# Gate products of the feed-forward by seven half-sized products instead of eight

## The chip, the cores and the metric

One core of a Trainium2 chip runs the whole program. The metric is device time in microseconds (us): the kernel before takes 1422.29 us, the median of 3 runs (1422.12 to 1422.38).

## The reference, cut to what matters

Two transformer-like blocks over 512 tokens of width 1024, in fp32. The change is in the last part of the second block, its gated feed-forward with 2816 hidden features:

```python
x = x + merged @ w_out[layer]
h = rmsnorm_2(x, norm_ffn[layer])
x = x + (jax.nn.silu(h @ w_ffn_gate[layer]) * (h @ w_ffn_up[layer])) @ w_ffn_down[layer]
```

Every large product must hold fp32 accuracy. `h @ w_ffn_gate` is 512 x 1024 times 1024 x 2816.

## The kernel before

**Products.** Everything is kept transposed: features on the 128 partitions, the 512 tokens in the free dimension, so a 1024-wide activation is 8 tiles of 128x512. Weights arrive in slabs of 1024 x 256 (8 inner tiles of 256 columns, 1 MB). A slab is split into two fp32r numbers: ScalarE writes the rounded high part (`split_hi`, L1146), VectorE the rest (`split_lo`, L1695); activations are split the same way. A product of two split numbers is three matmuls, high x high, high x low and low x high (`gemm`, L467). A slab gives two blocks of 128 outputs; a block is 8 inner tiles x 3 = 24 matmuls of 512 columns into one PSUM bank, and a slab is 48.

**Rings.** The raw slab, its high part and its low part each have 2 buffers. A slab is loaded when the low part of the slab two before is written, and split when TensorE has left the slab two before. SyncE issues all weight loads in program order.

**The end of `wout` (L2290 on VectorE, L1611 on ScalarE).** Four slabs, blocks k = 0 to 7. After each block VectorE adds it to the residual x (`add_to_x`, L2283), ScalarE multiplies x by the norm's gain and rounds it to `n_hi` (L1615) and squares x (L1603), VectorE writes the rest `n_lo` (L2288), GpSimd adds the squares (L2424). The root of their mean is needed only later, since the norm's factor is multiplied into the outputs (`RSTD`). TensorE starts the first feed-forward slab at once (`fup_part`, L1050): inner tiles 0 to 6 of both its blocks (42 matmuls), and only then tile 7 of both.

**The feed-forward.** Gate slab and up slab alternate (`fup0`, `fup1`, `fup2`: 4, 4 and 3 pairs), VectorE and ScalarE make silu(gate) x up of each and split it (L2316 to L2327), and after each chunk of 8 hidden tiles come the down slabs (`fdown0`, `fdown1`, each 4 slabs). The last 6 hidden tiles are `fdown2` and `fdown_end`; the last one's blocks are done by halves of 256 tokens (`end_block`, L1083).

**Order.** Each engine's program is written out by hand and an engine waits in order, on semaphores: what stands behind a waiting instruction waits as well.

Of the kernel before, what the change touches and what calls it, by code (L numbers as in the profile page):

```python
# [114 lines left out]
def build(nc, a, out):  # L115
# [79 lines left out]

    PH, s_at, b_at = {}, 0, 0
    for name, n, bps in [("in", 14, 2), ("pool_out", 2, 4), ("conv_out", 2, 4), ("wo", 4, 2)] + \
# [140 lines left out]
    def _(sp):
# [107 lines left out]
        run("fdown_end", w_d, k0=2 * KT, c0=3 * SLAB, kts=6)
# [9 lines left out]
    def _(pe):  # L456
# [587 lines left out]
        s0, _, b0, _ = PH["fup0"]  # L1044
        pe.wait_ge(S("lo_done"), s0 + 1)

        def fup_part(b, k):

            for n, (w, x) in enumerate(((hi_of, NHI), (hi_of, NLO), (lo_of, NHI))):
                mm = nc.tensor.matmul(G[(b0 + b) % 4][:], w(s0)[:, k, P * b:P * b + P], x[:, k, :],  # L1050
                                      start=k == 0 and n == 0, stop=k == KT - 1 and n == 2)
            return mm

        for b in range(2):
            pe.wait_ge(evac[(b0 + b) % 4], (b0 + b) // 4 + 1)
            for k in range(KT - 1):
                pe.wait_ge(S("ffn_in_lo"), k + 1)
                fup_part(b, k)
# [9 lines left out]
        gemm(s0 + 1, b0 + 3, range(KT), P, h(NHI), h(NLO))
        run("fup0", h(NHI), h(NLO), lo_slab=2, slabs=6)
        run("fup1", h(NHI), h(NLO))  # L1070
        run("fdown0", h(EHI[0]), h(ELO[0]), ready=h_ready(fbase))
        run("fup2", h(NHI), h(NLO))
        run("fdown1", h(EHI[1]), h(ELO[1]), ready=h_ready(fbase + KT))
        run("fdown2", h(EHI[0]), h(ELO[0]), kts=range(6), ready=h_ready(fbase + 2 * KT))

        def end_block(q):
# [1482 lines left out]
```

## Time and profile before

| what | value |
|---|---|
| median of 3 runs | 1422.29 us |
| the profiled execution's own time | 1422.33 us |
| its span in the trace | 1420.4 us |
| TensorE matmul busy | 1404.3 us, 99% of the span, 7223 matmuls |
| VectorE busy | 786.2 us, 55%, 1130 instructions |
| ScalarE busy | 538.5 us, 38%, 773 instructions |
| GpSimd busy | 167.1 us, 12% |
| TensorE clock granted, mean | 0.997 of full |

The times of instructions are from the start of the span. A matmul's listed duration (0.39 us for 512 columns) is longer than its pace, since one is under way while the next starts; the pace is the distance of two starts. On VectorE and ScalarE too an instruction may start some 0.08 us before the one ahead of it is listed as ended.

### The profile page before, as it was taken

Reading aid. Unit: us, or ns where it says so; the run is one execution under the profiler, and the core shown is the slowest. Engines: PE = TensorE matmul, PEld = TensorE weight load, DVE = VectorE, ACT = ScalarE, POOL = GpSimd, SP = SyncE. Lnnn points to the kernel's source line nnn. Section 1 sums busy time; section 2 is a strip of 40 time slices with the busy share of each in tenths; the row PEclk is TensorE's granted clock in tenths of the full one; section 3 lists DMA queues with packets and bytes.
Section 4 is the critical chain, followed back from the end, with each engine's and each line's share of the span. In section 5 each row is a group of like instructions: output and inputs, shape, how many; then the busy total and the mean of one; then the engine's idle time right before and its main releaser. Section 6 shows DMA issues by size and latency. Waiting matters only on the chain.

```text
span 1420.4 us, 17501 instructions
## 1 busy us (share of the span) xinstructions
PE 1404.3 (99%) x7223; PEld 1142.9 (80%) x7223; DVE 786.2 (55%) x1130; ACT 538.5 (38%) x773; POOL 167.1 (12%) x163
## 2 busy tenths in 40 slices
PE   7999999999999999999999999999999999999998
PEld 6888788988888888888888776668888888888887
DVE  6998674744234343378474666764545555435423
ACT  6232434643333132255453436662343223212214
POOL 1040013100000000120131711112210000000002
PEclk9999999999999999999999999999999999999999
DMA  6322224112322332323243212112322332332221
GB/s 200 116 89 90 89 89 148 61 60 89 119 89 90 101 103 92 96 90 97 89 90 119 73 60 60 30 31 76 103 90 89 108 100 90 97 111 89 90 89 60
DMA packets 136014, 129.67 MB, mean 91 GB/s; under 512 B 15776, under 2 KB 131424, under 8 KB 135904
## 3 DMA queue, kind: packets, MB, share of 16 engines
q1 hardware_dynamic: 134800, 124.90, 28.3%
q0 software_dynamic: 992, 3.47, 0.8%
q8 instruction: 57, 0.93, 0.3%
q10 hardware_dynamic: 144, 0.20, 0.0%
q14 instruction: 21, 0.17, 0.0%
HBM read 126.06 MB, written 2.10 MB: 90 GB/s over the span
## 4 chain that ended last, share of the span: by engine, by line
PE 95%; ACT 2%; DVE 1%; DMA 1%; issue 1%; SPq 0%; ACTq 0%
PE gemm L467 75%; PE gemm L586 3%; PE gemm L969 2%; PE misc L990 2%; PE misc L1009 1%; PE gemm L670 1%; PE gemm L617 1%; PE gemm L1050 1%; PE gemm L982 1%; PE misc L818 1%; DMA w_raw<-in_w_in 1%; PE misc L617 1%; PE gemm L495 1%; PE misc L982 1%; PE gemm L1083 1%
## 5 line engine op out<-in xcount | busy, mean ns | idle before, releaser
L1695 DVE TENSOR_TENSOR w_lo<-w_raw,w_hi 128x2048 fp32r<-128x2048 f32 (+1 forms) x108 | 245.8, 2276 | 174.6 <-ACT w_hi L1146 174.6
L467 PE MATMUL gemm<-h_hi,w_hi 128*128 128x512 f32 x828 | 324.8, 392 | 0.0
L467 PE MATMUL gemm<-h_hi,w_lo 128*128 128x512 f32 x828 | 322.3, 389 | 0.0
L467 PE MATMUL gemm<-h_lo,w_hi 128*128 128x512 f32 x828 | 322.3, 389 | 0.0
L1146 ACT ACTIVATE w_hi<-w_raw 128x2048 fp32r<-128x2048 f32 (+1 forms) x113 | 213.9, 1893 | 143.9 <-PE gemm L467 139.5
L467 PEld LDWEIGHTS gemm<-h_hi,w_hi 128*128 128x128 f32 x828 | 155.4, 188 | 35.2 <-issue 2.4
L467 PEld LDWEIGHTS gemm<-h_hi,w_lo 128*128 128x128 f32 x828 | 155.4, 188 | 32.6
L467 PEld LDWEIGHTS gemm<-h_lo,w_hi 128*128 128x128 f32 x828 | 155.5, 188 | 31.7 <-issue 0.2
L467 PE MATMUL gemm<-n_hi,w_hi 128*128 128x512 f32 x336 | 130.9, 390 | 0.0
L467 PE MATMUL gemm<-n_lo,w_hi 128*128 128x512 f32 x336 | 130.7, 389 | 0.0
L467 PE MATMUL gemm<-n_hi,w_lo 128*128 128x512 f32 x336 | 130.7, 389 | 0.0
L2424 POOL TENSOR_TENSOR sq_sum<-sq_sum,sq 128x512 f32<-128x512 f32 (+1 forms) x27 | 38.8, 1438 | 708.4 <-ACT sq L1603 365.3
L467 PE MATMUL gemm<-f_hi,w_hi 128*128 128x512 f32 x304 | 118.3, 389 | 0.0
L467 PE MATMUL gemm<-f_lo,w_hi 128*128 128x512 f32 x304 | 118.3, 389 | 0.0
L467 PE MATMUL gemm<-f_hi,w_lo 128*128 128x512 f32 x304 | 118.3, 389 | 0.0
L1785 DVE SCALAR_TENSOR_TENSOR conv_out<-v_padded,conv_cols,conv_out 128x512 f32<-128x512 f32 x120 | 89.8, 807 | 0.5
L467 PEld LDWEIGHTS gemm<-n_hi,w_hi 128*128 128x128 f32 x336 | 63.1, 188 | 13.3 <-issue 0.2
L467 PEld LDWEIGHTS gemm<-n_hi,w_lo 128*128 128x128 f32 x336 | 63.1, 188 | 13.1
L467 PEld LDWEIGHTS gemm<-n_lo,w_hi 128*128 128x128 f32 x336 | 63.1, 188 | 12.9
L467 PEld LDWEIGHTS gemm<-f_hi,w_lo 128*128 128x128 f32 x304 | 57.1, 188 | 11.9
L467 PEld LDWEIGHTS gemm<-f_hi,w_hi 128*128 128x128 f32 x304 | 57.1, 188 | 11.8
L467 PEld LDWEIGHTS gemm<-f_lo,w_hi 128*128 128x128 f32 x304 | 57.1, 188 | 11.8
(472 smaller groups left out, 1940.8 us busy)
## 6 DMA issues: line engine op xcount, KB each, us to landing
w_raw<-in_w_in SPq DMA_DIRECT2D x62, 512.0 KB, 4.6
w_raw<-in_w_down SPq DMA_DIRECT2D x32, 512.0 KB, 4.0
w_raw<-in_w_up SPq DMA_DIRECT2D x28, 512.0 KB, 4.3
w_raw<-in_w_ffn_gate SPq DMA_DIRECT2D x22, 512.0 KB, 4.5
w_raw<-in_w_ffn_up SPq DMA_DIRECT2D x22, 512.0 KB, 4.4
w_raw<-in_w_ffn_down SPq DMA_DIRECT2D x16, 512.0 KB, 4.2
w_raw<-in_w_o SPq DMA_DIRECT2D x8, 512.0 KB, 4.1
w_raw<-in_w_out SPq DMA_DIRECT2D x8, 512.0 KB, 4.1
```

The source lines that it names most:

```text
L467: mm = nc.tensor.matmul(bank[:], w(s)[:, kt, col0:col0 + P], x(n), start=first, stop=last)
L495: nc.tensor.matmul(G[(m + b) % 4][:], w(s)[:, k, P * b:P * b + P], HHI[:, k, :], start=k == 0 and w is hi_of, stop=False)
L586: mm = nc.tensor.matmul(G[m % 4][:], wide(w(s0 + j))[:, k, P * b:P * b + P], x[:, k, :], start=k == 0 and n == 0, stop=k == 3 and n == 2)
L617: mm = nc.tensor.matmul(bank[:, 0:HALF], w(s)[:, n // 3, P * (q % 2):P * (q % 2) + P], x[:, n // 3, SIDE[q // 2]], start=n == 0, stop=n == 23)
L670: nc.tensor.matmul(G[(m + b) % 4][:, SIDE[half]], w(s + b // 2)[:, k, P * (b % 2):P * (b % 2) + P], HHI[:, k, SIDE[half]], start=half == 0 ...
L969: mm = nc.tensor.matmul(G[bl % 2][:], w(s)[:, kt, P * (bl % 2):P * (bl % 2) + P], y[:, kt, :], start=x % 24 == 0, stop=x % 24 == 23)
L982: nc.tensor.matmul(banks[g][:, 0:w + P], QT[rows, q, w:w + P], KR[rows, i, 0:w + P], start=True, stop=True).then_inc(S("scores_full"), 1)
L990: mm = nc.tensor.transpose(bank[:, kb * P:(kb + 1) * P], PB[q % 2][:, g, kb * P:(kb + 1) * P], IDENT[:])
L1146: nc.scalar.activation(part(hi_of(s), s), part(raw_of(s), s), ACT.Copy).then_inc(S("hi_done"), SLABS_AT[s])
L1695: V.tensor_tensor(part(lo_of(s), s), part(raw_of(s), s), f(part(hi_of(s), s)), SUB).then_inc(S("lo_done"), SLABS_AT[s])
L1785: ins = V.scalar_tensor_tensor(y, x, w, y, MUL, ADD)
L2424: Q.tensor_tensor(SQA[:, cols], SQA[:, cols], SQ[j % 2][:, cols], ADD).then_inc(S("sq_added"), 1)
```

## The change

The 1024 x 256 gate slab is treated as a 2 x 2 matrix of halves: inner tiles even or odd, output columns 0 to 127 or 128 to 255. The activations are halved by the same inner tiles and by tokens 0 to 255 or 256 to 511. The four result quarters come from seven products in place of eight (Winograd's form): product p takes a half of the activations or a sum of such halves, and a half of the slab or a sum of such halves, 4 inner tiles x 3 = 12 matmuls of 256 columns each, 84 in all. The up and down slabs keep their products (48 matmuls of 512 columns to a slab).

Added around it:
- sums of the activations: 4 per pair of inner tiles (`input_sums`), once, in the `wout` loop. The activations now exist as 8 things to split (`ffn_in_hi`, `ffn_in_lo`), and ScalarE first writes x times gain in fp32 (`x_gained_pair`), then rounds it;
- sums of the weights: 4 operations per gate slab (`weight_sums`), three to `ffn_sums`, one in place in the raw slab, and the split of `ffn_sums` (1536 columns);
- sums of the products: ScalarE copies product 1 out of PSUM, VectorE does 7 additions of 256 columns (`join_*`), then the multiplication by RSTD (`scale`). The products rotate through the four `misc` banks;
- raw and low parts share a buffer and have a ring of 3, the high parts a ring of 2; loads wait for the slab three before;
- down slabs come in chunks of four hidden tiles (`fdown_0` to `fdown_3` behind gate and up slabs 3, 5, 7 and 9, 2 slabs of 4 blocks each), 8 `add_to_x` per chunk: 32 in place of 16.
Several GpSimd semaphores before this stage are merged into one (`gpsimd_prepared`), with the same waits.

Where TensorE takes up the feed-forward, w = 0:

```diff
+        def product(w, p, first=0, last=4):
+            f_ = W_SLAB[w]
+            if first == 0:
+                pe.wait_ge(S("lo_done"), SPLIT_AT[f_] + PART_OF[p])
+                n = done_at(w, p) - 5
+                if n >= 0:
+                    pe.wait_ge(*p_read(n // 7, ORDER[n % 7]))
+            bank, a_ = p_bank(w, p), LEFT_OF[p]
+            for pair in range(first, last):
+                if w == 0:
+                    pe.wait_ge(S("ffn_in_part"), 4 * pair + {1: 1, 2: 3}.get(p, 4))
+                hi = right_of(FHI_[f_ % 2], FSUMH[w % 2], p, pair)
+                lo = right_of(FLO_[f_ % 3], FSUML[w % 2], p, pair)
+                for n, (w_, x) in enumerate(((hi, AHI), (hi, ALO), (lo, AHI))):
+                    mm = nc.tensor.matmul(bank[:, 0:HALF], w_, x[:, a_, pair, :], start=pair == 0 and n == 0,
...
+        product(0, 1)
+        for p in (6, 7, 5, 2):
+            product(0, p, 0, 3)
+        for p in (6, 7, 5, 2):
+            product(0, p, 3, 4)
...
+        for w in range(1, N_W):
+            for p in ORDER:
+                product(w, p)
+            for b in range(2):
+                up_block(w, b)
+            if w in LAST_W[0:4]:
+                for j in range(2):
+                    for b in range(4):
+                        down_block(LAST_W.index(w), j, b)
```

ScalarE and VectorE in the `wout` loop:

```diff
         for k in range(KT):
-            if k % 2 == 0:
+            pair = k // 2
+            if k in (0, 2, 4):
                 split_hi(s0 + k // 2 + 1)
+            if k == 4:
+                even_hi(0)
+            if k == 5:
+                sums_hi(0)
+                odd_hi(0)
             if k == KT - 1:
                 A_(TMP16[:, 0:1], EPSB[:], ACT.Sqrt)
-                split_hi(s0 + 5)
+                down_hi(1)
             act.wait_ge(*evac_at(b0 + k))
-            A_(NHI[:, k, :], XT[:, k, :], ACT.Copy, scale=col("norm_ffn_2", k)).then_inc(S("ffn_in_hi"), 1)
-            last(k, b0 + k, 0)
+            if k >= 2:
+                act.wait_ge(S("ffn_in_part"), 4 * (pair - 1) + 3)
+            A_(XGN[:, k % 2, :], XT[:, k, :], ACT.Copy, scale=col("norm_ffn_2", k)).then_inc(S("x_gained"), 1)
+            act.wait_ge(S("x_gained"), k + 1)
...
+                act.wait_ge(S("ffn_in_part"), 4 * pair + 2)
+                A_(AHI[:, 4:8, pair, :], ASUM[:, :, pair, :], ACT.Copy).then_inc(S("ffn_in_hi"), 1)
...
         for k in range(KT):
-            if k:
-                ffn_in_lo(k - 1)
+            if k in (0, 2, 4):
+                split_lo(s0 + k // 2 + 1)
+            if k == 3:
+                weight_sums(0, 0)
+                weight_sums(0, 1)
+            if k == 4:
+                even_lo(0)
+            if k == 5:
+                sums_lo(0)
+                odd_lo(0)
+            add_to_x(k, b0 + k, 0)
             if k % 2 == 0:
-                split_lo(s0 + k // 2 + 1)
-            if k == KT - 1:
-                split_lo(s0 + 5)
-            add_to_x(k, b0 + k, 0)
-        ffn_in_lo(KT - 1)
+                input_lo(k // 2, 0)
+            else:
+                input_sums(k // 2)
+                input_lo(k // 2, 1)
+                input_lo(k // 2, 2)
```

VectorE in the feed-forward, for one w:

```diff
+        for w in range(N_W):
+            f_, open_ = W_SLAB[w], w and w - 1 not in LAST_W
+            if open_:
+                gated(w - 1, 1)
+                act_lo(w - 1, 0)
+            up_lo(f_ + 1, 0)
+            join_u2(w)
+            up_lo(f_ + 1, 1)
+            join_u3(w)
...
+            join_u4_c22(w)
+            if w and f_ + 2 in W_OF:
+                weight_sums(w + 1, 0)
+            join_c11(w)
...
+            join_c12(w)
...
+            join_c21(w)
...
+            scale(w)
+            if f_ + 2 in W_OF:
+                even_lo(f_ + 2)
+                sums_lo(f_ + 2)
+                odd_lo(f_ + 2)
+            else:
+                down_lo(f_ + 2)
+            silu(w, 0)
+            silu(w, 1)
+            gated(w, 0)
```

How this moves instructions is seen in the built programs, read engine by engine. First VectorE at the end of the `wout` loop, from block k = 4 to k = 7; `x_T` is the residual, `n_lo` and `ffn_in_lo` the low part of the normed activations. Before:

```order
L2288 SCALAR_TENSOR_TENSOR n_lo<-x_T,param_cols,n_hi 128x512 [waits ffn_in_hi]
L2283 TENSOR_TENSOR x_T<-x_T,gemm 128x512 [waits block_full]
L2288 SCALAR_TENSOR_TENSOR n_lo<-x_T,param_cols,n_hi 128x512 [waits ffn_in_hi]
L1695 TENSOR_TENSOR w_lo_57<-w_raw_53,w_hi_55 128x2048 [waits hi_done]
L2283 TENSOR_TENSOR x_T<-x_T,gemm 128x512 [waits block_full]
```

And after, from the addition of block 5 to that of block 7:

```order
L2505 TENSOR_TENSOR x_T<-x_T,gemm 128x512 [waits block_full]
L2549 TENSOR_TENSOR ffn_in_sums<-x_gained_pair 128x256 [waits x_gained]
L2550 TENSOR_TENSOR ffn_in_sums<-x_gained_pair 128x256
L2552 TENSOR_TENSOR ffn_in_sums<-ffn_in_sums,x_gained_pair 128x256 [waits vector_step]
L2554 TENSOR_TENSOR ffn_in_sums<-x_gained_pair,ffn_in_sums 128x256 [waits vector_step]
L2563 TENSOR_TENSOR ffn_in_lo<-x_gained_pair,ffn_in_hi 128x2x256 [waits ffn_in_hi]
L2566 TENSOR_TENSOR ffn_in_lo<-ffn_in_sums,ffn_in_hi 128x4x256 [waits ffn_in_hi]
L2505 TENSOR_TENSOR x_T<-x_T,gemm 128x512 [waits block_full]
L2560 TENSOR_TENSOR ffn_in_lo<-x_gained_pair,ffn_in_hi 128x2x256 [waits ffn_in_hi]
L2505 TENSOR_TENSOR x_T<-x_T,gemm 128x512 [waits block_full]
```

Between two additions of the residual stood one short operation, and now up to six, two of which wait for ScalarE; the addition of the next block stands behind them.

ScalarE for block k = 7, the last, and what stands ahead of it. Before:

```order
L1603 ACTIVATE sq_74<-x_T 128x512 [waits sq_added,evacuated1]
L1612 ACT_TABLE_LOAD
L1612 ACTIVATE pool_head<-eps 128x1
L1146 ACTIVATE w_hi_54<-w_raw_52 128x2048 [waits block_full,raw_ready0]
L1615 ACTIVATE n_hi<-x_T,param_cols 128x512 [waits evacuated2]
```

And after:

```order
L1755 ACTIVATE sq_74<-x_T 128x512 [waits sq_added,evacuated1]
L1801 ACT_TABLE_LOAD
L1801 ACTIVATE pool_head<-eps 128x1
L1789 ACTIVATE ffn_hi_202<-ffn_raw_196 128x2048 [waits raw_ready1,block_full]
L1806 ACTIVATE x_gained_pair<-x_T,param_cols 128x512 [waits ffn_in_part,evacuated2]
L1812 ACTIVATE ffn_in_hi<-x_gained_pair 128x2x256 [waits x_gained]
L1816 ACTIVATE ffn_in_hi<-ffn_in_sums 128x4x256 [waits ffn_in_part]
```

The table load and the 2048-column split stood in this place already; behind them the one operation on block 7 has become three in a row of waits.

TensorE behind the last `wout` block, w = 0. The first matmuls of product 1 and of product 6, after the change (before, 42 matmuls of 512 columns stood ahead of the first one that needs inner tile 7):

```order
L1143 MATMUL misc<-ffn_in_hi,ffn_hi_201 128x256 [waits ffn_in_part,lo_done]
L1143 MATMUL misc<-ffn_in_lo,ffn_hi_201 128x256
L1143 MATMUL misc<-ffn_in_hi,ffn_lo_198 128x256
...
L1143 MATMUL misc<-ffn_in_hi,ffn_sums_hi_207 128x256 [waits ffn_in_part,lo_done]
L1143 MATMUL misc<-ffn_in_lo,ffn_sums_hi_207 128x256
L1143 MATMUL misc<-ffn_in_hi,ffn_sums_lo_205 128x256
```

Product 1 needs the last pair's even tile (k = 6) behind 9 matmuls; the pair's sums (k = 7) are needed 39 matmuls after that.

## Rows read from the trace of the kernel before

**Rows 1.** The page: busy time by engine, and the chain that ended last.

```profile
PE 1404.3 (99%) x7223; PEld 1142.9 (80%) x7223; DVE 786.2 (55%) x1130; ACT 538.5 (38%) x773; POOL 167.1 (12%) x163
PE 95%; ACT 2%; DVE 1%; DMA 1%; issue 1%; SPq 0%; ACTq 0%
```

**Rows 2.** Chain in order of time, from 1000 us: start, us, what.

```profile
1049.30 10.88 PE gemm L1050 x48
...
1063.94 337.99 PE gemm L467 x1491
```

**Rows 3.** Timeline, TensorE: first and last of 54 half-width matmuls in a row.

```profile
1401.76 0.28 PE L1083 MATMUL gemm<-h_hi,w_hi 128*128 128x256 f32 x1
...
1408.11 0.28 PE L1083 MATMUL gemm<-h_hi,w_lo 128*128 128x256 f32 x1
```

**Rows 4.** Timeline, TensorE, end of wout: the matmuls that follow blocks 5 and 7.

```profile
1038.26 0.39 PE L467 MATMUL gemm<-h_hi,w_hi 128*128 128x512 f32 x1
...
1049.13 0.39 PE L1050 MATMUL gemm<-n_hi,w_hi 128*128 128x512 f32 x1
```

**Rows 5.** Timeline, VectorE, wout: start, duration, instruction, idle before it.

```profile
1016.70 0.69 DVE L2283 TENSOR_TENSOR x_T<-x_T,gemm 128x512 f32<-128x512 f32 x1 [1.51 <-PE gemm L467]
...
1042.27 2.29 DVE L1695 TENSOR_TENSOR w_lo<-w_raw,w_hi 128x2048 fp32r<-128x2048 f32 x1 [1.58 <-ACT w_hi L1146]
1044.47 0.68 DVE L2283 TENSOR_TENSOR x_T<-x_T,gemm 128x512 f32<-128x512 f32 x1
1045.95 0.75 DVE L2288 SCALAR_TENSOR_TENSOR n_lo<-x_T,param_cols,n_hi 128x512 fp32r<-128x512 f32 x1 [0.79 <-ACT n_hi L1615]
```

**Rows 6.** Timeline, ScalarE, wout.

```profile
1039.81 0.62 ACT L1603 ACTIVATE sq<-x_T 128x512 f32<-128x512 f32 x1
1040.33 1.91 ACT L1146 ACTIVATE w_hi<-w_raw 128x2048 fp32r<-128x2048 f32 x1
1045.19 0.72 ACT L1615 ACTIVATE n_hi<-x_T,param_cols 128x512 fp32r<-128x512 f32 x1 [2.96 <-DVE x_T L2283]
1045.82 0.62 ACT L1603 ACTIVATE sq<-x_T 128x512 f32<-128x512 f32 x1
1046.45 1.28 ACT L1612 ACT_TABLE_LOAD   x1
1047.75 0.20 ACT L1612 ACTIVATE pool_head<-eps 128x1 f32<-128x1 f32 x1
```

**Rows 7.** Timeline, VectorE and ScalarE, first gate block.

```profile
1065.95 0.63 ACT L1633 ACTIVATE sq<-h_now 128x512 f32<-128x512 f32 x1
1066.61 0.69 DVE L2318 SCALAR_TENSOR_TENSOR h_now<-sq,h_now 128x512 f32<-128x512 f32 x1 [0.70 <-ACT sq L1633]
1067.34 0.69 DVE L2320 TENSOR_TENSOR h_now<-h_now,rstd 128x512 f32<-128x512 f32 x1
1067.95 0.68 DVE L2316 TENSOR_TENSOR h_now<-gemm,rstd 128x512 f32<-128x512 f32 x1
```

**Rows 8.** Groups of VectorE by shape: busy, mean ns of one, idle before.

```profile
L1943 DVE TENSOR_TENSOR x_T<-x_T,y_T 128x256 f32<-128x256 f32 x32 | 12.9, 414 | 0.0
L1695 DVE TENSOR_TENSOR w_lo<-w_raw,w_hi 128x1536 fp32r<-128x1536 f32 x4 | 7.0, 1759 | 7.2 <-ACT w_hi L1146 7.2
```

**Rows 9.** Timeline, GpSimd, the same stretch of wout.

```profile
1040.50 1.34 POOL L2424 TENSOR_TENSOR sq_sum<-sq_sum,sq 128x512 f32<-128x512 f32 x1 [3.53 <-ACT sq L1603]
```

**Rows 10.** The tile q_rope: min, median and max ns of one.

```profile
L2162 DVE TENSOR_TENSOR q_rope<-q_rope,sin x4: 684/686/1573, 811.5 to 819.8; 128x512 f32<-128x512 f32 x4
```

**Rows 11.** Timeline, TensorE at 829 us.

```profile
828.94 0.63 PE L911 MATMUL gemm<-h_lo,w_hi 128*128 128x512 f32 x1
...
831.08 0.48 PE L911 MATMUL gemm<-h_hi,w_hi 128*128 128x512 f32 x1
```

**Rows 12.** Windows: busy us (and instructions) by engine, granted clock.

```profile
828.00:830.00 2.00, 2.00 (x8) 1.65 (x9) 1.49 (x4) 2.00 (x2) 0.00 (x0) 0.50 0.05 12
1100.00:1200.00 100.00, 100.00 (x443) 82.83 (x442) 53.36 (x58) 28.28 (x28) 0.00 (x0) 1.00 0.31 97
```

More of the change, by code:

```diff
@@ L1043, in _ @@
         fbase = H2 + 2 * KT
[L1044 to L1058, printed above, removed]
@@ new lines, in last_down @@
+        def last_down(j, b, first, last):
+            f_, m = PH["fdown2"][0] - SF + j, PH["fdown2"][2] + 2 * j + b
+            if first == 0:
+                pe.wait_ge(S("lo_done"), SPLIT_AT[f_] + 1)
+                pe.wait_ge(evac[m % 4], m // 4 + 1)
+            for n in range(first, last):
+                k, (w, x) = n // 3, ((FHI_[f_ % 2], ACTH), (FHI_[f_ % 2], ACTL), (FLO_[f_ % 3], ACTH))[n % 3]
+                if j == 0 and n % 3 == 0:
+                    pe.wait_ge(S("hlo_ready"), fbase + 16 + k + 1)
+                mm = nc.tensor.matmul(G[m % 4][:], w[:, k, P * b:P * b + P], x[:, k, :], start=n == 0, stop=n == 17)
+            if last == 18:
+                mm.then_inc(S("block_full"), 1)
@@ L1068, in _ @@
[L1068 to L1074, printed above, removed]
+        mean_rows(SQ[1][:], False, True, F_MEAN).then_inc(S("mean_ready"), 1)
+        product(0, 3)
@@ L1076, in end_block @@
+        last_down(0, 1, 0, 12)
+        last_down(0, 0, 12, 18)
+        last_down(0, 1, 12, 18)
+        for j in (1, 2):
+            for b in range(2):
+                last_down(j, b, 0, 18)
+        E_SLAB = N_SLABS - 1 - SF
         def end_block(q):
@@ L1279, in _, with root_of_rows @@
             nc.scalar.activation(Y[:, k, cols], G[m % 4][:, cols], ACT.Copy).then_inc(evac[m % 4], 1)
-        def root_of_rows(n, root=None):
+        def root_of_rows(n, root=None, bank=M[0]):
             act.wait_ge(S("mean_ready"), n)
@@ L1642, in _ @@
+        act_hi(N_W - 1, 1)
         s0, _, b0, _ = PH["fdown2"]
@@ new lines, in _, with input_sums @@
+        X11, X12, X21, X22 = (XGN[:, b, SIDE[half]] for half in range(2) for b in range(2))
+        def input_sums(pair):
+            dve.wait_ge(S("x_gained"), 2 * pair + 2)
+            s1, s2, s3, s4 = (ASUM[:, n, pair, :] for n in range(4))
+            step.inc(V.tensor_tensor(s1, X21, X22, ADD))
+            V.tensor_tensor(s3, X11, X21, SUB)
+            step.wait(dve)
+            step.inc(V.tensor_tensor(s2, s1, X11, SUB))
+            step.wait(dve)
+            V.tensor_tensor(s4, X12, s2, SUB).then_inc(S("ffn_in_part"), 1)
@@ new lines, in silu, with gated @@
+        def silu(w, b):
+            dve.wait_ge(S("ffn_tanh"), 2 * w + b + 1)
+            step.inc(V.scalar_tensor_tensor(FGATE[:, b, :], SQ[b][:], 1.0, FGATE[:, b, :], ADD, MUL))
+            step.wait(dve)
+            step.inc(V.tensor_tensor(FGATE[:, b, :], FGATE[:, b, :], RSTD[:], MUL))
+        def gated(w, b):
+            m = PH[f"fup{w}"][2] + b
+            full(m)
+            step.wait(dve)
+            V.tensor_tensor(FUP[:, b, :], FGATE[:, b, :], G[m % 4][:], MUL).then_inc(evac[m % 4], 1)
```

403 lines of the change are left out of this document (305 added, 98 removed).

## The prediction

> **What bounds the kernel now.** I read the page first: TensorE has a matmul under way for 99% of the span and holds 95% of the chain that ended last [rows 1]. Busy says little by itself, since matmuls overlap, so I read that chain in order of time over the stage that changes. From 1063.94 us it is one unbroken piece of 1491 matmuls in 337.99 us, 0.2267 us each, and the 48 ahead of it take 10.88 us [rows 2]: the same pace, no wait anywhere. VectorE is 53% busy there and ScalarE 28% [rows 12]. So in the feed-forward only the matmul stream counts, as long as the others keep up, and every us that TensorE waits is added to the end.
>
> **The term that shrinks.** A gate slab is 48 x 0.2267 = 10.88 us. After the change it is 84 matmuls of 256 columns. Their pace stands in the trace: 54 in a row start from 1401.76 to 1408.11 us, 6.35 / 53 = 0.1198 us [rows 3], across three blocks and their waits. So 84 x 0.1198 = 10.06 us and the slab saves 0.82 us, not the 1.36 us that an eighth of 10.88 would be: of a half-width matmul 0.0131 us is overhead (2 x 0.1198 - 0.2267). Eleven slabs save **9.0 us**. Up slabs (528 matmuls) and down slabs have as many as before, and I take the old pace for them.
>
> **What is added beside TensorE, in the steady stretch.** One w is 10.06 + 10.88 = 20.94 us of TensorE. VectorE's prices, from start to next start: 512 columns 0.61, or 0.73 where the next waits for the result [rows 7]; 2048 columns 2.20 [rows 5]; so about 0.07 + 1.04 per 1000 columns, which fits 256 and 1536 columns (listed 0.41 and 1.76, less the 0.08 overlap: 0.34 and 1.67) [rows 8] and gives 1.14 for 1024. Per w: up slab's low part 2.3, seven joins 2.4, weight sums 2.7, scale 1.2, low parts of the next gate slab 1.14 + 1.67 + 1.14, silu 2.7, gated 1.2, activations' low part 1.2: 17.6 us of 20.94. It is much fuller than now, with little room for waits, but placed against the times: joins of the products at 4 to 11 us of the w, next slab's parts written by about 17, gated at 19. A product's bank is wanted back three products (4.3 us) later. Behind w = 3, 5, 7 and 9 come 96 down matmuls, 21.8 us, against 8 additions and two low parts, some 9 us. I cost all this at nothing; the cover is 3 us a w. The last four hidden tiles' factors come two w later than they are made, so the down blocks wait for nothing; at the end 24 matmuls (5.4 us) cover the last tile.
>
> **What is on the path: the start.** Before, VectorE and ScalarE did a block k of `wout` in about 2.2 us and idled until the next; block 5.44 us. Now their work per block is a chain of waits through both engines, with the next addition queued behind it. Prices between engines, start to start: addition to ScalarE 0.72 (1044.47 to 1045.19), ScalarE's gained copy to whoever waits 0.76 (1045.19 to 1045.95) [rows 5, 6], a plain 512 copy 0.66 [rows 7] and 0.52 to the next on ScalarE (1039.81 to 1040.33), the 2048 split 1.94 until VectorE starts [rows 5, 6] and 1.80 to the next on ScalarE; in between by the same slope 1024 columns 0.95 and 1.09, 1536 columns 1.38 and 1.52. Followed from block 1's addition at 1016.70 [rows 5]:
> - k = 1: addition and gained copy 0.72 + 0.76, four sums 0.34 + 0.34 + 0.46 + 0.46 = 1.60, ScalarE rounds the sums 0.95: 1020.7.
> - k = 2: slab split 1.94 + 2.20, addition, gained copy and rounding 0.72 + 0.76 + 0.66, low part 0.61: 1027.6.
> - k = 3: weight sums 0.73 + 0.61 + 0.73 + 0.61, then as k = 1, 4.03: 1034.3.
> - k = 4: split 4.14: the last `wout` slab is ready at 1038.55, and due at 1038.26 [rows 4]: TensorE waits **0.3 us**. Even low part 1.14, addition and copies 0.72 + 0.76, rounding and square 1.04: 1042.1.
> - k = 5: sums' high part 1.52, low parts 1.67 + 1.14, then 0.72 + 0.76 + 1.60, rounding 1.09, low part 1.14: 1051.7.
> - k = 6: 0.72 + 0.76 + 0.66 + 0.73: the even tile is there at **1054.6**. ScalarE is free at 1054.35 (rounding 0.52, square 0.63 [rows 6]).
> - k = 7: on ScalarE the table load and root, 1.50 [rows 6], and the 2048 split, 1.80, stand ahead, then 0.76 + 1.60 + 1.09 + 1.26: the last sums are there at **1062.4**.
>
> TensorE finishes `wout` at 1049.13 [rows 4] + 0.3, does 9 matmuls of product 1 (1.1 us) and waits at 1050.5 until 1054.6: 4.1 us. Then 3 + 36 matmuls, 4.7 us, and a wait from 1059.3 to 1062.4: 3.1 us. Before, 42 matmuls of 0.2267 = 9.5 us covered the one tile of block 7; now 5.8 us of matmuls cover it, and the work ends 13 us behind TensorE. Sum of waits **7.5 us**. The norm's factor is late next, its mean is 4 matmul groups further back; I find it just in time: rows inverted at about 1067.2 where TensorE comes to it.
>
> **GpSimd in the same stretch.** Each square is added by GpSimd in 1.34 us, 0.69 us after the square starts [rows 9, 6]; VectorE has little to do then, and now is at its sums. One of four q_rope operations, next to GpSimd work, took 1573 ns in place of 686 [rows 10], 0.89 us more. If one VectorE operation on the chain is held for a GpSimd addition, it costs up to 1.34 us; four places can meet (k = 1, 2, 3, 5): 0 to 5.4 us. By the computed starts the square's addition comes within 0.1 us of an operation at each, and at k = 2 it meets the weight sums squarely. I take **1.0 us**.
> The Trainium skill (SBUF — State Buffer, section SBUF: two separate sides) says that a VectorE operation with two SBUF inputs and a GpSimd operation that reads SBUF exclude each other for a whole instruction. By it every overlap costs its full remainder, and with two overlaps the sum would be some 1423, an estimate. The q_rope row agrees in kind.
>
> **Sum.** 1422.3 - 9.0 + 7.5 + 1.0 = **1421.8 us**. The durations are of an execution of 1422.33 us (span 1420.4 and 1.9 around it, which the change leaves alone), within 0.04 us of the median, so nothing is scaled. 0.2% is 2.8 us, about what a measurement tells from no change. Bounds of the start's waits: a change of the chain's end moves them one for one. The listed durations without the 0.08 us overlap, on some 38 steps, give 10.5; hand-overs (0.12 to 0.14 us each, some 25) for nothing give 4.5.
>
> **Rivals.**
> 1. *The start's waits are small, under 6 us in all* (1413.3 with none, 1419.4 at 6). For it: my hand-over prices come from a few rows, and free hand-overs would do it (4.5). Against: of the 35.1 us from k = 1 to k = 5 some 32 are bare work, 6.4 us a block against TensorE's 5.44. 0.20.
> 2. *The start costs over 12 us, or the clock falls* (slower, 1425.2 to 1428). The place is the first products; it decides when waits plus clock exceed 11.8 us. At 829 us the granted clock was 0.50, the 1.2 GHz level, and 512-column matmuls then started 0.428 us apart (5 in 2.14 us) [rows 11, 12], 0.20 us more each; a stretch like that of 2.7 us costs 1.35, behind a run of 64 small matmuls. Two waits of 3 to 4 us could bring it down twice; the first slow stretch is hidden in the second wait, the second costs 1.3 to 1.9 in full. With all four GpSimd meetings too: 1422.3 - 9.0 + 7.5 + 5.4 + 1.9 = 1428.1. 0.15.
> The clock alone, 1421.8 + 1.3 to 1.9, gives 1423.1 to 1423.7 and stays in case 4; a chance of 0.4 that a slow stretch shows at all. The Trainium skill (TensorE: Matmul & The Clock Gate, HAM oscillation) says that idle gaps between bursts of matmuls put TensorE back to half its clock. The feed-forward before has no gap that could show it.
> 3. *VectorE becomes the bound, or the up slab's activations, now read in two pieces of 256 columns, cost TensorE per piece* (slower). If every VectorE step costs a quarter more, 22.0 us a w against 20.94, 1.1 us for each of the 6 w's without down work: 6.6. If each of 528 matmuls pays the 0.0131 us overhead twice: 6.9. Either gives 1428.5. For it: 17.6 us of 20.94 with about eight waits between engines. Against: the bank slack, and that no row shows a strided operand costing. 0.13.
> 4. *The forecast*: waits between 6.2 and 11.8, 1419.5 to 1425.1. 0.52.
>
> **Numbers.** Faster 0.20 (rival 1), same 0.52, slower 0.28 (rivals 2 and 3). The range of 8 in 10 reaches halfway into rival 1 and up to the lower edge of rival 3's price: 1416.5 to 1428.
>
> **What would show each step.** Right: in the page TensorE's chain broken after `wout`, a wait of about 4 us at the fourth pair of product 1 and of about 3 at the fourth pair of product 6, both released by VectorE's `ffn_in_lo`; from there to 1400 us no wait over 0.3; first matmuls of two gate slabs 20.94 us apart; half-width pace 0.120. VectorE some 85% busy in w = 1 to 3. Wrong: VectorE's low parts later than a product's first matmul in w = 1 to 3; an up matmul's pace over 0.23; a granted clock of 0.5 after 1050 us.
> What would make it wrong above all is the chain's length: it is nearly 50 steps, and 0.05 us on each is 2.5 us.

## The result and the profile after

The changed kernel takes 1424.86 us (median of 20 runs, 1421.88 to 1425.27) against 1422.39 us (20 runs, 1420.60 to 1424.45): ratio **1.0016**, 95% interval 1.0010 to 1.0022. It is about 2.5 us slower. The prediction's 1421.8 us was 0.5 us on the other side of the kernel before; the measured time lies in its range and within the 0.2% that it called no change.

The page of the changed kernel, span, busy time by engine, and the chain that ended last (before: [rows 1]):

```profile
span 1423.0 us, 18658 instructions
PE 1399.6 (98%) x7619; PEld 1157.7 (81%) x7619; DVE 882.7 (62%) x1320; ACT 565.8 (40%) x818; POOL 167.2 (12%) x163
...
PE 93%; DVE 3%; ACT 2%; issue 1%; DMA 1%; SPq 0%; ACTq 0%
```

TensorE is under way 4.7 us less, and the span is 2.6 us longer: some 7 us of new gaps. The waits of TensorE from 1000 us (total, times, longest) say where they are; before there were none:

```profile
PE misc L1143 <- DVE ffn_in_lo L2560: 4.3, 1, 4.3
PE misc L1143 <- issue: 1.9, 1, 1.9
PE gemm L542 <- DVE w_lo L1917: 1.3, 1, 1.3
```

The chain in order of time, from those waits on (start, us, what; before: [rows 2]):

```profile
1056.23 5.34 PE misc L1143 x30
1061.57 1.89 issue
1063.46 4.25 PE misc L1143 x21
1067.71 0.57 PE gemm L591 x16
1068.28 3.07 PE misc L1143 x24
1071.35 0.89 PE gemm L598 x8
1072.24 10.93 PE gemm L1159 x48
1083.17 10.07 PE misc L1143 x84
1093.24 10.91 PE gemm L1159 x48
...
1337.27 21.76 PE gemm L1175 x96
...
1380.01 24.48 PE gemm L1189 x108
```

Two things are to be seen. From 1072.24 us there is no wait: a gate slab of 84 matmuls takes 10.07 us and an up slab 10.91, 20.98 us a w where it was 21.76 [rows 2]. And in the first products 30 matmuls take 5.34 us and 21 take 4.25, where 0.1198 us each [rows 3] would be 3.6 and 2.5. (Such a row ends with the last matmul's listed end; where none is slow, the same 30 and 21 have rows of 3.86 and 2.74 us, as runs below show.) TensorE's timeline shows why, behind the first and behind the second wait (weight loads):

```profile
1056.23 0.19 PEld L1143 LDWEIGHTS misc<-ffn_in_hi,ffn_hi 128*128 128x128 f32 x1 [4.46 <-DVE ffn_in_lo L2560]
...
1057.15 0.33 PEld L1143 LDWEIGHTS misc<-ffn_in_lo,ffn_sums_hi 128*128 128x128 f32 x1
1057.37 0.33 PEld L1143 LDWEIGHTS misc<-ffn_in_hi,ffn_sums_lo 128*128 128x128 f32 x1
...
1063.43 0.19 PEld L1143 LDWEIGHTS misc<-ffn_in_hi,ffn_hi 128*128 128x128 f32 x1 [2.06 <-issue]
...
1064.02 0.34 PEld L1143 LDWEIGHTS misc<-ffn_in_lo,ffn_hi 128*128 128x128 f32 x1
1064.23 0.33 PEld L1143 LDWEIGHTS misc<-ffn_in_hi,ffn_lo 128*128 128x128 f32 x1
```

From 1056.93 to 1060.14 us and again from 1063.80 to 1067.00 us a matmul starts every 0.214 us, and a weight load takes 0.33 us in place of 0.19. The granted clock there is 0.50, the lower of the two levels (1.2 GHz); windows of TensorE, with length, busy us, count, granted clock, DMA:

```profile
1057.00:1060.00 3.00, 3.00 (x16) 0.50 0.00 0
1063.90:1067.00 3.10, 3.10 (x16) 0.50 0.00 0
```

The mean granted clock of the execution is 0.995, before 0.997.

The second wait has no releaser in the waits' view ("issue"), so I looked at what ends beside it on ScalarE:

```profile
1055.99 1.28 ACT L1801 ACT_TABLE_LOAD   x1
...
1057.39 1.89 ACT L1789 ACTIVATE ffn_hi<-ffn_raw 128x2048 fp32r<-128x2048 f32 x1
...
1061.52 1.06 ACT L1816 ACTIVATE ffn_in_hi<-ffn_in_sums 128x1024 fp32r<-128x1024 f32 x1 [0.96 <-DVE ffn_in_sums L2554]
1062.48 0.61 ACT L1755 ACTIVATE sq<-x_T 128x512 f32<-128x512 f32 x1
1063.00 0.36 ACT L1824 ACTIVATE copy_p<-misc 128x256 f32<-128x256 f32 x1
```

`copy_p` takes product 1 out of its bank. The products rotate over four banks, so the fifth one begun, product 2, has to wait for that copy (`pe.wait_ge(*p_read(n // 7, ORDER[n % 7]))`, with n = 0). The count of matmuls confirms the place: between 1056.23 and 1063.43 us stand 30 matmuls, the last 3 of product 1 and 27 of products 6, 7 and 5; the prediction had 3 + 36 there.

Last, VectorE in `wout`, the same instruction with and without a GpSimd addition beside it (here k = 1, 3 and 5, then k = 7):

```profile
1019.66 1.78 DVE L2563 TENSOR_TENSOR ffn_in_lo<-x_gained_pair,ffn_in_hi 128x512 fp32r<-128x512 f32 x1
...
1034.34 1.79 DVE L2563 TENSOR_TENSOR ffn_in_lo<-x_gained_pair,ffn_in_hi 128x512 fp32r<-128x512 f32 x1
...
1050.50 1.79 DVE L2563 TENSOR_TENSOR ffn_in_lo<-x_gained_pair,ffn_in_hi 128x512 fp32r<-128x512 f32 x1
...
1061.40 0.68 DVE L2563 TENSOR_TENSOR ffn_in_lo<-x_gained_pair,ffn_in_hi 128x512 fp32r<-128x512 f32 x1
```

With the first of the weight sums at k = 2 (1.79 us at 1027.63), all four possible meetings happened, at 1.1 us each.

### The profile page after: what moved, and what is told of

Read it like the earlier page. It is cut to its first block, busy times and chain, and to the rows that moved or that the text cites. A ratio compares the mean times of both kernels' runs of the same rounds, so it can differ in the third digit from the quotient of the medians.

```text
span 1423.0 us, 18658 instructions
## 1 busy us (share of the span) xinstructions
PE 1399.6 (98%) x7619; PEld 1157.7 (81%) x7619; DVE 882.7 (62%) x1320; ACT 565.8 (40%) x818; POOL 167.2 (12%) x163
## 4 chain that ended last, share of the span: by engine, by line
PE 93%; DVE 3%; ACT 2%; issue 1%; DMA 1%; SPq 0%; ACTq 0%
PE gemm L542 49%; PE gemm L1159 8%; PE misc L1143 8%; PE gemm L1175 6%; PE gemm L661 3%; PE gemm L1044 2%; PE gemm L1189 2%; PE misc L1065 2%; PE misc L1084 1%; PE gemm L745 1%; PE gemm L692 1%; PE gemm L1057 1%; PE misc L893 1%; DMA w_raw<-in_w_in 1%; PE misc L692 1%
## 5 line engine op out<-in xcount | busy, mean ns | idle before, releaser
L542 PE MATMUL gemm<-h_hi,w_hi 128*128 128x512 f32 x728 | 286.0, 393 | 1.3 <-DVE w_lo L1917 1.3
L542 PE MATMUL gemm<-h_hi,w_lo 128*128 128x512 f32 x728 | 283.5, 389 | 0.0
L542 PE MATMUL gemm<-h_lo,w_hi 128*128 128x512 f32 x728 | 283.4, 389 | 0.0
L1917 DVE TENSOR_TENSOR w_lo<-w_raw,w_hi 128x2048 fp32r<-128x2048 f32 x74 | 170.0, 2298 | 133.3 <-ACT w_hi L1298 133.0
L1298 ACT ACTIVATE w_hi<-w_raw 128x2048 fp32r<-128x2048 f32 x79 | 150.7, 1908 | 72.7 <-PE gemm L542 68.3
L1789 ACT ACTIVATE ffn_hi<-ffn_raw 128x2048 fp32r<-128x2048 f32 (+1 forms) x23 | 42.3, 1840 | 82.3 <-PE misc L1143 37.4
L1159 PE MATMUL gemm<-ffn_in_hi,ffn_hi 128*128 128x512 f32 x176 | 68.7, 390 | 0.0
L1159 PE MATMUL gemm<-ffn_in_lo,ffn_hi 128*128 128x512 f32 x176 | 68.6, 390 | 0.0
L1159 PE MATMUL gemm<-ffn_in_hi,ffn_lo 128*128 128x512 f32 x176 | 68.5, 389 | 0.0
L1143 PE MATMUL misc<-ffn_in_hi,ffn_hi 128*128 128x256 f32 x176 | 50.8, 289 | 6.2 <-DVE ffn_in_lo L2560 4.3
```

Source lines behind the costliest of these rows:

```text
L542: mm = nc.tensor.matmul(bank[:], w(s)[:, kt, col0:col0 + P], x(n), start=first, stop=last)
L1143: mm = nc.tensor.matmul(bank[:, 0:HALF], w_, x[:, a_, pair, :], start=pair == 0 and n == 0, stop=pair == 3 and n == 2)
L1159: mm = nc.tensor.matmul(G[m % 4][:].rearrange("p (a n) -> p a n", n=HALF), w_[:, k, P * b:P * b + P], x[:, a_:a_ + 2, k // 2, :], start=k ...
L1298: nc.scalar.activation(part(hi_of(s), s), part(raw_of(s), s), ACT.Copy).then_inc(S("hi_done"), SLABS_AT[s])
L1789: A_(part(FHI_[f_ % 2], SF + f_), part(FRAW[f_ % 3], SF + f_), ACT.Copy).then_inc(S("hi_done"), 1)
L1917: V.tensor_tensor(part(lo_of(s), s), part(raw_of(s), s), f(part(hi_of(s), s)), SUB).then_inc(S("lo_done"), SLABS_AT[s])
```

## The experiments

Theory 1: the products give their gain in full, and the start loses it, by waits and by the lower clock behind them. Against it stood a steady loss (theory 2) and GpSimd as the cause (theory 3). Profiled executions reach `wout` up to 3.4 us apart, so spans are compared from one mark, the first low part of a slab in `wout` (`w_lo`, at 1010.77 us in the changed kernel), to the end. This difference goes with the granted clock in a stage that none of the runs changes: from 828 to 834 us it is 1.00 in the four runs with marks from 1009.1 to 1009.4, and 0.50 for a part of the stretch in all others, longest in the two with marks at 1012.5. The medians mix executions with early and late marks, so a difference of 1 to 2 us between two medians need not come from the change. Each kernel has one trace, so a difference from the mark is of two executions. "First up" is the first weight load of the first up slab, from the same mark.

| kernel | median us | ratio to before (95%) | span | mark | mark to end | first up |
|---|---|---|---|---|---|---|
| before | 1422.4 | 1 | 1420.4 | 1010.76 | 409.6 | |
| changed | 1424.9 | 1.0016 (1.0010-1.0022) | 1423.0 | 1010.77 | 412.2 | 61.2 |
| reordered | 1417.9 | 0.9967 (0.9954-0.9979) | 1416.0 | 1010.70 | 405.3 | 54.3 |
| no GpSimd adds | 1422.3 | 1.0000 (0.9991-1.0009) | 1421.6 | 1012.46 | 409.1 | 58.1 |
| table early | 1420.5 | 0.9989 (0.9980-0.9998) | 1420.7 | 1011.46 | 409.2 | 58.2 |
| kept busy | 1427.9 | 1.0034 (1.0021-1.0046) | 1426.4 | 1011.09 | 415.3 | 64.3 |
| reordered, bank | 1415.1 | 0.9950 (0.9938-0.9963) | 1415.6 | 1012.48 | 403.1 | 52.1 |
| bank early | 1422.2 | 1.0000 (0.9991-1.0009) | 1419.5 | 1009.40 | 410.1 | 59.1 |
| kept busy, both | 1423.6 | 1.0008 (0.9999-1.0017) | 1420.1 | 1009.38 | 410.7 | 59.7 |
| reordered, joins | 1415.2 | 0.9950 (0.9938-0.9963) | 1411.6 | 1009.11 | 402.5 | 51.4 |
| sums late | 1416.0 | 0.9951 (0.9937-0.9964) | 1411.0 | 1009.17 | 401.8 | 50.8 |

**Reordered.** ScalarE's and VectorE's `wout` loops are written as lists of steps (sh, sl: split of the next slab; table: Sqrt table load; add: addition to the residual; xg, ah, ahs: gained copy, rounding, rounding of sums; sq: square; S: input sums; lo0 to lo11: input low parts; ws: weight sums; eh, suh, oh and el, sul, ol: parts of gate slab 0; dh1: up slab's split).

```diff
+        for item in ("sh1 table0 xg0 ah0 sq0 sq1 xg1 ah1 sh2 ahs0 xg2 ah2 sq2 xg3 sh3 sq3 "
+                     "eh0 suh0 ah3 ahs1 xg4 sq4 oh0 ah4 xg5 ah5 ahs2 sq5 sq6 xg6 ah6 xg7 "
+                     "ah7 ahs3 dh1 sq7 ").split():
...
+        for item in ("sl1 add0 add1 lo0 S0 ws0 sl2 add2 lo1 lo2 lo3 add3 S1 ws1 sl3 add4 "
+                     "lo4 lo5 add5 lo6 el0 sul0 ol0 S2 lo7 add6 lo8 lo9 add7 S3 lo10 lo11 ").split():
```

> Same work as the changed kernel; only ScalarE's and VectorE's instructions of the wout stage stand in another order (the Sqrt table load right after the first weight split, the split of the first up slab behind the last input copies, the sums' and up pieces moved between the blocks), so that TensorE should find its operands ready. Theory 1 (the products give the whole gain, some 0.8 us a gate slab; it is lost in the start's waits, 1.3 + 4.3 + 1.9 us, and in matmuls at the lower clock behind two of them, 1.7 us each): the three waits are gone and the clock stays up, the span falls by about 11 us against the changed kernel, to 1412 (ratio to the kernel before 0.994, about 1414 us). Theory 2 (the gain of the products is eaten in the steady stretch, by VectorE or by the slower two-piece operand, or the wait comes back at the first joins): the span stays above 1418, with new waits after 1075 us. Theory 3 (the meetings with GpSimd move with the order and cost what they cost): one or two waits of 1 to 2 us remain, 1414 to 1416.

The waits for `w_lo` and `ffn_in_lo` are gone and the gain is 6.9 us from the mark, but the span is 1416.0 us and not 1412, since one wait is left:

```profile
PE misc L1143 <- issue: 2.7, 1, 2.7
```

Its chain, and ScalarE beside it:

```profile
1049.25 4.67 PE misc L1143 x39
1053.91 2.71 issue
1056.62 4.12 PE misc L1143 x21
```

```profile
1053.84 1.89 ACT L1789 ACTIVATE ffn_hi<-ffn_raw 128x2048 fp32r<-128x2048 f32 x1
1056.16 0.36 ACT L1821 ACTIVATE copy_p<-misc 128x256 f32<-128x256 f32 x1
```

Again the wait stands ahead of the last 21 matmuls of the first five products, though the inputs are there (the last low part is written from 1053.97 to 1055.20 us): TensorE's weight load comes at 1056.59, 0.43 us behind the start of the copy. In the changed kernel it was 1063.00 to 1063.43, the same 0.43. Theory 2 falls: from the first up slab's first weight load (1065.00 us) to the last stage's (1397.13) are 332.13 us, as in the changed kernel (1071.97 to 1404.10). The time is in the range that theory 3 gave; that the wait is the bank's and not GpSimd's is shown by the run with the bank copy early, further down.

**No GpSimd adds.**

```diff
-            Q.memset(SQA[:], 0.0).then_inc(S("sq_added"), 1)
+            Q.memset(SQA[:], 1.0 if n == 2 else 0.0).then_inc(S("sq_added"), 1)
...
-                Q.tensor_tensor(SQA[:, cols], SQA[:, cols], SQ[j % 2][:, cols], ADD).then_inc(S("sq_added"), 1)
+                if n == 2:
+                    Q.memset(SQA[:, 0:1], 1.0).then_inc(S("sq_added"), 1)
+                else:
+                    Q.tensor_tensor(SQA[:, cols], SQA[:, cols], SQ[j % 2][:, cols], ADD).then_inc(S("sq_added"), 1)
```

> The changed kernel, with the seven 128x512 adds by which GpSimd sums the squares in the wout stage replaced by writes of one element: the sum of squares is left out, so the feed-forward's norm is computed from other numbers. If the four VectorE instructions of 1.8 us (0.69 us elsewhere) are stretched by those adds, all four take 0.7 us now. Theory 1 with the meetings as a part of the chain: the wait of the last wout slab (1.3 us) is gone and the two waits at the last pair fall by 1 to 2 us together; the span falls by 2.5 to 3.5 us, to 1420. Rival, that the stretch lies beside other waits of VectorE and costs nothing: span as before, 1423. Rival, that GpSimd is the whole loss: span 1412.

All four instructions take 0.7 us, so the additions did stretch them. From the addition of block 1 to the start of the last low part, VectorE needs 44.3 us (1018.40 to 1062.69) in place of 45.9 (1016.71 to 1062.61): of 4.4 us of stretch only 1.6 were on the chain. At k = 1 and k = 3 they lay beside ScalarE's split of the next slab, for which VectorE waits in this run:

```profile
1024.37 2.29 DVE L1917 TENSOR_TENSOR w_lo<-w_raw,w_hi 128x2048 fp32r<-128x2048 f32 x1 [0.58 <-ACT w_hi L1298]
```

The kernel gained 3.1 us from the mark, because the second slow stretch did not come either, behind a wait of the same length (chain):

```profile
1056.32 5.35 PE misc L1143 x30
1061.67 1.88 issue
1063.55 2.74 PE misc L1143 x21
```

So 1.6 us was the stretch, 1.5 the clock; theory 3 has a part, not the whole.

**Table early.**

```diff
+            if k == 0:
+                A_(TMP16[:, 0:1], EPSB[:], ACT.Sqrt)
...
-                A_(TMP16[:, 0:1], EPSB[:], ACT.Sqrt)
```

> The changed kernel with one step moved: ScalarE's Sqrt table load (1.28 us, between blocks 6 and 7, ahead of the 2048-element split and of block 7's copies) stands right behind the first weight split of the wout stage. If ScalarE at the last block is on the chain that sets the end of the wait (theory 1), the waits at the last pair fall by 1.2 to 1.5 us together, and the span by as much, to 1421.6; if VectorE alone is (rival), nothing changes, and if the block it now stands ahead of takes the delay, the wout wait grows by up to 1.3 us and the span stays at 1423.

It gives 3.0 us from the mark, twice what was expected. The second wait is gone: TensorE, slowed behind the first for 20 matmuls (16 in the changed kernel), reaches product 2 at 1062.67 us, and the copy, 1.5 us earlier from the mark, began at 1062.18. With no second wait there is no second slow stretch. The median of 1420.5 us is 1.9 under the kernel before, but from the mark it is only 0.4 (409.2 and 409.6): seven of the eleven executions lie at 1420.2 to 1420.6 us with a mean granted clock of 0.998, the other four, the profiled one among them, at 1422.2 to 1422.5 with 0.995.

**Kept busy.** Matmuls whose results are dropped, into a free bank.

```diff
+        def keep_busy(n, i):
+            bank = G[PH["fup0"][2] % 4]
+            pe.wait_ge(*evac_at(PH["fup0"][2] - 4))
+            for j in range(n):
+                nc.tensor.matmul(bank[:, 0:HALF], HHI[:, j % KT, 0:P], HHI[:, 4 + i, 0:HALF], start=True, stop=True)
...
-        product(0, 1)
+        product(0, 1, 0, 3)
+        keep_busy(34, 0)
+        product(0, 1, 3, 4)
         for p in (6, 7, 5, 2):
             product(0, p, 0, 3)
+        keep_busy(26, 1)
```

> The changed kernel with 34 and 26 matmuls of 256 columns, whose results are dropped, ahead of the last pair of the first product and of the last pairs of the next four: work in place of the two waits. The chain of VectorE and ScalarE is as it was. If the slow matmuls (0.21 us apart against 0.12) behind the two waits come from TensorE's idle time, they run at 0.12 us now; the first slow stretch lies ahead of a wait and gives nothing, the second gives 1.4 to 1.7 us: span 1421.5, ratio to the kernel before 1.0005. Rival, that the slow pace has another cause: both stretches stay at 0.21 us and the span at 1423 or, with the added matmuls at the slow pace, above it.

The forecast was missed: from the mark it is 3.1 us slower than the changed kernel. The first fillers did their work: behind them 30 matmuls take 3.86 us, none slow. But the second wait grew to 3.4 us, its end as before, and the second fillers stood behind it, 9 matmuls after its end, and were all cost. This is what showed that the wait is not at the last pairs but ahead of product 2.

**Reordered, bank copy early.**

```diff
-                     "ah7 ahs3 dh1 sq7 ").split():
+                     "ah7 cp0 ahs3 dh1 sq7 ").split():
...
-        copy_p1(0)
```

> The reordered kernel (span 1416.0) with one step more moved: ScalarE's copy of product 1 out of its PSUM bank stands ahead of the rounding of the last sums, where ScalarE idles 0.96 us, in place of behind the up slab's split and the last square. In the reordered kernel TensorE still waited 2.7 us, in the middle of the first products, and began again 0.2 us behind the start of that copy. Theory 1, now as a wait for the PSUM bank (the fifth product, 2, goes to product 1's bank): the wait of 2.7 us and the slow matmuls behind it (1.6 us) are gone, the span is 1411.7 to 1412.7 (up to 1 us may come back where product 3 waits for the bank of product 6, whose join stands behind the up slab's low part); ratio to the kernel before 0.994. Rival, that this wait is for the last input copies: it stays at 2 us or more and the span at 1415 to 1416.

The wait of 2.7 us and the slow stretch are gone, so it was the bank's. (From the copy's start to TensorE's next weight load it had been 0.43 us, not 0.2.) Waits of 0.8 and 0.4 us came back at the last input low parts, so only 2.2 us of the expected 3.3 to 4.3 were won (405.3 to 403.1 from the mark). VectorE's waits name a cause further up, in the middle of `wout`, where the reordered loop asks for gate slab 0 earlier than the changed kernel does; in the reordered run the same wait was 1.0 us:

```profile
DVE ffn_sums L2531 <- DMA ffn_raw<-in_w_ffn_gate: 2.1, 1, 2.1
```

**Bank copy early alone.**

```diff
+                if k == KT - 1:
+                    copy_p1(0)
                 act.wait_ge(S("ffn_in_part"), 4 * pair + 2)
...
-        copy_p1(0)
```

> The changed kernel with that one step alone moved: the copy of product 1 ahead of the last sums' rounding (from 1063.0 to about 1060.6 us). If the second wait is for the bank, TensorE does the first nine matmuls of product 2 from about 1061.3 us and then waits until the last sums' low part at 1063.9, with 12 matmuls behind it in place of 21: the span falls by 1.2 us with full clock behind the wait, by up to 2.3 if the slow stretch is shorter too; 1420.7 to 1421.8. Rival, that the last sums' low part ends the wait already: no change, 1423.

2.1 us from the mark, within the forecast of 1.2 to 2.3. The second wait now has a releaser in the waits' view, and it is the one that I had forecast, the last sums' low part; behind it stand 12 matmuls at full pace (chain):

```profile
PE misc L1143 <- DVE ffn_in_lo L2561: 4.3, 1, 4.3
...
PE misc L1143 <- DVE ffn_in_lo L2567: 1.2, 1, 1.2
```

```profile
1062.51 1.70 PE misc L1143 x12
```

**Kept busy, both waits.**

```diff
-        product(0, 1)
+        product(0, 1, 0, 3)
+        keep_busy(34, 0)
+        product(0, 1, 3, 4)
         for p in (6, 7, 5, 2):
+            if p == 2:
+                keep_busy(25, 1)
             product(0, p, 0, 3)
```

> The changed kernel with 34 matmuls of dropped result ahead of the last pair of product 1, and 25 ahead of product 2, where the second wait stands (the run before had them behind it, where they could only add time). If TensorE's idle time is what brings the slow matmuls, none starts over 0.13 us behind the one before it from 1050 to 1068 us, and the 21 matmuls behind the second wait take 2.5 us in place of 4.25: span 1421.3, ratio to the kernel before 1.0005. Rival: slow matmuls behind the waits in spite of it, 1423 or over.

No slow matmul is left, and the 21 take 2.74 us (chain):

```profile
1054.84 3.86 PE misc L1143 x30
1058.70 3.00 PE gemm L1155 x25
1061.69 0.38 issue
1062.08 2.74 PE misc L1143 x21
```

The granted clock over this stretch (window) is full:

```profile
1054.84:1068.00 13.16, 12.78 (x114) 1.00 0.01 1
```

1.5 us from the mark, with the chain of VectorE and ScalarE untouched (the second wait ends 52.7 us behind the mark in both): in this execution the slow matmuls of the changed kernel go with TensorE's idle time and not with what it computes. The first slow stretch was hidden: the run before with fillers removed it, and the second wait grew by as much. The second cost 1.5 us.

**Reordered, joins first.**

```diff
-                     "ah7 cp0 ahs3 dh1 sq7 ").split():
+                     "ah7 cp0 ahs3 sq7 dh1 ").split():
...
+            if w == 0:
+                join_u2(w)
+                join_u3(w)
             up_lo(f_ + 1, 0)
-            join_u2(w)
+            if w:
+                join_u2(w)
             up_lo(f_ + 1, 1)
-            join_u3(w)
+            if w:
+                join_u3(w)
```

> As the run with reordered steps and the early bank copy, and two steps more moved for the first w alone: the last square ahead of the up slab's split on ScalarE, and the first two joins ahead of the up slab's low parts on VectorE, so that product 3 finds its bank read. Theory 1: no wait over 0.3 us is left between 1000 and 1400 us, span 1411.5, ratio to the kernel before 0.9935 to 0.994; against the run with the bank copy alone 0 to 1 us less. Rival (a steady loss): span over 1415 with waits after 1075 us.

Waits of TensorE, from 1000 to 1400 us:

```profile
PE gemm L598 <- DVE rstd_rows L2147: 0.5, 1, 0.5
PE misc L1143 <- DVE ffn_in_lo L2562: 0.4, 1, 0.4
```

Two waits over 0.3 us are left, against the forecast; the span of 1411.6 us is as forecast, but of the 4.0 us by which it is under that of the reordered kernel with the early bank copy alone 3.4 are its early mark. From the mark it is 0.6 us less than that run, with no difference in the medians (1415.2 and 1415.1). Both are some 7.2 us faster than the kernel before, ratio 0.995. VectorE waits 1.1 us for gate slab 0's transfer here (2.1 us in that run), so most of the 0.6 us can be that and not the joins.

**Sums late.** ScalarE's and VectorE's lists:

```diff
+        for item in ("sh1 table0 xg0 sq0 ah0 xg1 ah1 sq1 ahs0 sh2 xg2 sq2 ah2 xg3 sq3 ah3 "
+                     "sh3 ahs1 eh0 xg4 suh0 sq4 oh0 ah4 xg5 ah5 ahs2 sq5 xg6 ah6 sq6 dh1 "
+                     "xg7 ah7 sq7 cp0 ahs3 ").split():
...
+        for item in ("sl1 add0 add1 lo0 S0 lo1 lo2 sl2 add2 ws0 add3 lo3 S1 lo4 ws1 sl3 "
+                     "add4 lo5 el0 sul0 add5 lo6 ol0 S2 add6 lo7 lo8 lo9 add7 S3 lo10 lo11 ").split():
```

> As the run before (reordered, bank copy early, joins first), with the orders changed once more: gate slab 0's weight sums stand behind the low part of wout slab 2 and block 2's addition, some 5 us later, and the up slab's split stands ahead of block 7's copies. In the last two runs VectorE waited 1.1 and 2.1 us at the first weight sum for the transfer of gate slab 0, and in the second of them every later step was 1.1 us behind the first reordered run. If that transfer was what brought the last 1 to 2 us of waits back, VectorE does not wait for it now, no wait over 0.3 us stands before product 3, and from the mark to the end it is 401 to 401.8 us (402.5 and 403.1 before), span about 1411 by the same start; median 1414 to 1415. Rival: the squares' additions on GpSimd fall on other VectorE steps now and cost the same 1 us: 402.5 or over.

VectorE no longer waits for a transfer, and TensorE does the first five products, 60 matmuls, without a stop (the chain's row of the last 51, and TensorE's only wait from 1000 to 1400 us):

```profile
1047.72 6.13 PE misc L1143 x51
```

```profile
PE gemm L598 <- DVE rstd_rows L2147: 0.5, 1, 0.5
```

From the mark it gains 7.8 us on before and 10.4 on the changed kernel. GpSimd's additions still stretched five VectorE instructions, to 1.0 to 1.8 us, and TensorE waited for none of them. The run moved several steps at once, so how much each gave is not shown. The median of 1416.0 us missed the forecast of 1414 to 1415; in the medians of five runs each (1416.0, 1415.2, 1415.1) this kernel, the one before it and the reordered one with the early bank copy can't be told apart.

## Why the prediction was off by 3.1 us, point by point

- **The gain.** Forecast 9.0 us, measured 11 x (21.76 - 20.98) = 8.6. The products cost what was predicted (10.07 against 10.06); the up slab went from 10.88 to 10.91. It is there in full: from the first weight load of the first up slab to that of the last stage the kernel before needs 1401.54 - 1060.68 = 340.9 us, of which 0.9 are eight small matmuls that the changed kernel does ahead of that slab, and the changed kernel 332.1, so 7.8 us less over the ten later w. The run without the start's waits gains 7.8 us from the mark, with 0.5 us of wait left.
- **VectorE and the operand in two pieces (rival 3).** Refuted: no wait in any w, and 332.13 us from the first up slab to the last stage in the changed and in the reordered kernels.
- **The chain of VectorE and ScalarE.** 4.1 us forecast for the first wait, 4.3 measured. The last low part was computed to be there at 1062.4 us, before GpSimd's 1.0, and was there at 1062.61 + 1.23 = 1063.8; without the GpSimd additions, counted from the same mark, at 1062.2. So the chain itself was computed right to 0.2 us, by some luck with nearly 50 steps.
- **GpSimd.** I took 1.0 us, and all four meetings happened. Taking them away shortened the chain by 1.6, 0.6 more than I took. That is also where the `wout` wait of 1.3 us (forecast 0.3) comes from: 0.2 us without the additions. The Trainium skill (SBUF — State Buffer, section SBUF: two separate sides) says that such a pair excludes each other for a whole instruction. The traces agree on the instruction (0.69 to 1.79 us); its price on the chain was 1.6 us and not the sum of 4.4.
- **The step that failed: "Then 3 + 36 matmuls, 4.7 us, and a wait from 1059.3 to 1062.4".** Product 2 had to wait for product 1's bank after 3 + 27 matmuls. The prediction costed the banks at nothing because they are wanted back three products (4.3 us) later; at w = 0 only 27 matmuls of those products stand between, 3.2 us at full pace, and the copy stands on ScalarE behind everything that block 7 needs. With the wait there, 21 matmuls stand behind it in place of 12, 1.1 us, of which 0.4 comes back since it ends 0.4 us ahead of the last low part: 0.7 us. And the clock was low behind it, 1.5 us more. The copy moved alone gives both back, 2.1 of the 3.1 us of the miss. That the bank ends the wait is shown by that run (waits 1.9 to 1.2, 9 matmuls done ahead) and by the 0.43 us from the start of the copy to TensorE's weight load in the five runs that have this wait. That the waits at the start summed to 7.5 us in forecast and measurement (1.3 + 4.3 + 1.9) is luck: a part of what should have been wait was spent in slow matmuls.
- **The clock, left out of the sum** at a chance of 0.4 and priced 1.3 to 1.9 us: this is the second term that was missing. It fell twice, the first was hidden as foreseen, the second cost 1.5 us, by keeping TensorE busy and by the rows (21 matmuls in 4.25 us against 2.74). The Trainium skill (TensorE: Matmul & The Clock Gate, section HAM oscillation) says that idle gaps between bursts bring half the clock; the traces agree behind every wait of 2.7 us and more (six waits in six runs), and behind one of the two waits of 1.9 us.

Start to finish: forecast -9.0 + 7.5 + 1.0 = -0.5. Measured: gain -8.6; `wout` wait 1.3; first wait 4.3; 30 matmuls 1.7 longer than 0.1198 us each; second wait 1.9; 21 matmuls 1.7 longer (some 0.2 of each 1.7 is the last matmul's listed end and not the clock): 2.3 of the 2.6 us by which the span grew. The 0.3 left are not accounted for. Term by term against the forecast: the gain 0.4 us smaller, GpSimd 0.6 more, the rest of the chain 0.2 less, the place of the second wait 0.7, the clock 1.5: 3.0 of the 3.1 us from -0.5 to +2.6.

## What to carry to other kernels

When a loop's head waits for a chain of short instructions, list every semaphore of each TensorE step, the accumulators' release too, and look where the releasing copy stands in its engine's queue: here product 1 was done at some 1056.9 us and the copy began at 1063.0, behind a split of 1.9 us and a square of 0.6 that could have waited, among other work. A wait of some us on TensorE here also cost what followed it at the lower clock, so removing one short cause (a table load of 1.28 us) gave back twice its length here. A change that shortens the steady part can be judged by the pace there and the start by itself; this one was worth 7 us once its start was ordered anew.

## What the runs showed of the hardware that was not expected

- The clock did not follow the length of the wait alone: behind 1.9 us it was 0.50 in the changed kernel, with 1.0 us of matmuls at full pace ahead of the wait, and stayed up without the GpSimd adds, with 1.7 us of them. Behind the one of 1.2 us and the one of 0.8 us it stayed up.
- A GpSimd addition of 128x512 beside a VectorE instruction of 0.69 us made that one 1.79 us long, and itself 1.47 to 1.49 us at three of the four places where alone it is 1.29.
- Matmuls with the moving operand in two pieces of 256 columns run at 0.2273 us (10.91 / 48) against 0.2267 (21.76 / 96, down slabs) in one piece: 0.6 ns.
